# First projections of four RMS-normalized layers fed with un-normalized rows, rotary tables moved, and 20 scaling pieces placed later

## What is computed

```
x = x + conformer_conv_mixer(rms_norm(x, a_norm[0]), ...)      # a0
x = x + forgetting_attention_mixer(rms_norm(x, b_norm), ...)   # b
x = x + short_conv_mixer(rms_norm(x, c_norm), ...)             # c
x = x + conformer_conv_mixer(rms_norm(x, a_norm[1]), ...)      # a1
for l in range(2):                                             # m0 f0 m1 f1
    mod = silu(c) @ w_ada[l] + b_ada[l]          # scale, shift, gate vectors
    x = layer_norm(ALPHA * x + g1 * token_mixer(x * (1 + sc1) + sh1, ...))
    x = layer_norm(ALPHA * x + g2 * conv_ffn(x * (1 + sc2) + sh2, ...))
```

## Time and profile before

| | before |
|---|---|
| median of 3 runs | 1755.38 us (1754.99 to 1758.14) |
| the profiled execution | 1757.02 us, span 1755.1 us |
| PE busy | 1723.7 us (98%) |
| DVE busy | 1477.8 us (84%) |
| ACT busy | 1093.9 us (62%) |
| POOL busy | 289.3 us (16%) |
| DMA | 339.49 MB, mean 193 GB/s |

### The profile page before, as it was taken

The page is one execution under the profiler, slowest core; times in us unless marked ns, Lnnn a source line. Parts: engine busy times, 40 slices in busy tenths (PEclk is TensorE's granted clock), DMA queues, the critical chain, the costliest instruction groups (busy, mean ns, idle before and its releaser), DMA issues.

```text
span 1755.1 us, 28782 instructions
## 1 busy us (share of the span) xinstructions
PE 1723.7 (98%) x10458; PEld 1510.9 (86%) x10458; DVE 1477.8 (84%) x2862; ACT 1093.9 (62%) x2150; POOL 289.3 (16%) x396
## 2 busy tenths in 40 slices
PE   9999999999999999999999999999999999999997
PEld 8888888888888888788898988988888998988886
DVE  7998878877789999888987698789987688789887
ACT  6888665555455555577876455566566656566664
POOL 3996000000000000088920000002000200002000
PEclk9999999999999999999999999999999999999999
DMA  6455568855559888544465654546764544546662
GB/s 240 153 157 174 168 220 304 268 177 184 201 195 315 292 301 309 177 151 144 145 196 157 233 172 133 172 150 187 258 218 144 168 156 130 172 144 187 221 187 78
DMA packets 92734, 339.49 MB, mean 193 GB/s; under 512 B 10288, under 2 KB 10672, under 8 KB 91952
## 3 DMA queue, kind: packets, MB, share of 16 engines
q1 hardware_dynamic: 92592, 337.64, 59.1%
HBM read 336.55 MB, written 1.05 MB: 192 GB/s over the span
## 4 chain that ended last, share of the span: by engine, by line
PE 74%; DVE 12%; ACT 8%; issue 4%; POOL 2%; ACTq 0%; DVEq 0%; POOLq 0%
PE ps L104 72%; DVE wl L120 4%; ACT tmp L110 3%; ACT wh L113 2%; POOL B L120 2%; PE ps L107 2%; DVE tmp L130 1%; DVE raw L130 1%; DVE tmp L120 1%; DVE B L120 1%; ACT os L113 1%; DVE sm L142 1%; DVE os L120 1%; ACT B L110 0%; DVE tmp L125 0%
## 5 line engine op out<-in xcount | busy, mean ns | idle before, releaser
L104 PE MATMUL ps<-XS,wh 128*128 128x256 f32 (+2 forms) x3184 | 780.7, 328 | 8.5 <-DVE wl L120 4.4
L120 DVE TENSOR_TENSOR wl<-raw,wh 128x1024 fp32r<-128x1024 f32 x471 | 576.6, 1238 | 101.4 <-ACT wh L113 99.1
L104 PE MATMUL ps<-XS,wl 128*128 128x256 f32 x2152 | 583.1, 282 | 0.0
L104 PEld LDWEIGHTS ps<-XS,wh 128*128 128x128 f32 (+1 forms) x3184 | 527.0, 191 | 64.9 <-issue 19.0
L113 ACT CAST wh<-raw 128x1024 fp32r<-128x1024 f32 x471 | 479.3, 1044 | 100.3 <-PE ps L104 92.8
L104 PEld LDWEIGHTS ps<-XS,wl 128*128 128x128 f32 x2152 | 409.4, 190 | 11.4
L120 POOL TENSOR_TENSOR B<-B,tmp 128x236 f32<-128x236 f32 (+11 forms) x368 | 247.0, 712 | 640.0 <-ACT tmp L110 625.1
L104 PE MATMUL ps<-wh,os 128*128 128x512 f32 x864 | 280.2, 392 | 4.1 <-DVE os L120 2.8
L130 DVE SCALAR_TENSOR_TENSOR ps<-B,C,ps 128x253 f32<-128x253 f32 (+17 forms) x560 | 216.5, 472 | 2.8 <-ACT ps L110 2.8
L104 PE MATMUL ps<-B,raw 128*128 128x256 f32 x992 | 218.6, 380 | 0.0
L104 PEld LDWEIGHTS ps<-B,raw 128*128 128x128 f32 x992 | 187.0, 190 | 27.2 <-issue 2.9
(11 more groups left out here) (168 smaller groups left out, 1659.7 us busy)
## 6 DMA issues: line engine op xcount, KB each, us to landing
raw<-in_w SPq DMA_DIRECT2D x628, 512.0 KB, 4.4
B<-in_ln SPq DMA_DIRECT2D x4, 1024.0 KB, 7.7
C<-in_cst SPq DMA_DIRECT2D x1, 1103.5 KB, 9.0
X<-in_x SPq DMA_DIRECT2D x2, 512.0 KB, 4.5
out_x<-X SPq DMA_DIRECT2D x4, 256.0 KB, 2.5
cb<-in_cb SPq DMA_DIRECT2D x1, 512.0 KB, 13.6
pos<-in_pos SPq DMA_DIRECT2D x1, 160.0 KB, 5.3
raw<-in_w SPq DMA_DIRECT2D x1, 128.0 KB, 2.0
```

What stands on the lines that cost most here:

```text
L104: return NOTHING if self.e is None else self.e.matmul(*a, **k)
L120: return NOTHING if self.e is None else self.e.tensor_tensor(o, a, b, op)
```

## The change

- Entry of b, c and a1: the quarters of the layer before are finished in the order (0,0), (1,0), (0,1), (1,1). Ahead of the last one PE transposes the first four feature blocks of the *un-normalized* rows, and the other four are transposed inside the first unit. The fillers of these entries go, and 6 of the 24 at the start of a0. The normalizing of the rows ahead of the transposes goes too.
- a0 and a1: g0 (two plain units) is made from the un-normalized rows times the gain; DVE multiplies its result by R. R is spread over the partitions with two matmuls (`pe_row_root`), ACT copies it to SBUF, and DVE makes the normalized blocks from the un-normalized ones. v0 of a1 becomes plain.
- b: v0 comes ahead of b.f and takes un-normalized high and low parts; R is applied as its result leaves PSUM. The same eight blocks are then made again, normalized and split, for v1 and the rest. b.f goes behind v1, and the small work on its result moves to the chunks v2 and k0.
- c: the c and u units of the first step take un-normalized rows; their product is multiplied by R*R. The blocks are made again, normalized and split, for the b and z units.
- The masks of a0 (four) are made ahead of the convolution and not within its first step. The rotary tables are made on DVE and ACT behind output pieces of a1 and not at the start of a0.
- Scaling pieces: 31 instead of 36 in b, 38 instead of 46 in c (fewer at its start, and in its last step two instead of six), 12 instead of 8 in m0 (one behind each of iq0 to iq3 too), 4 instead of 6 in f0 (at steps 18 and 20 instead of 8 to 12), 11 instead of none in m1 (behind iq0 to iq2 and qk0 to qk7).

The diff, cut to its core:

```diff
     for p in range(8):
-        first = "split" if j else "plain"
-        two("g", p, E, *[first if p == 1 else "plain"] * 2)
-        two("v", p, 0, "split" if p else first, "plain" if p else first)
+        two("g", p, E, *["split" if j and p == 1 else "plain"] * 2)
+        two("v", p, 0, "split" if p else "plain", "plain")
         if p in EARLY_Z:
             out += z_unit(EARLY_Z.index(p))
     for x in range(len(EARLY_Z), 16):
...
-    out = [("b.f", [("b_w_in", 0, 128 * k, 128, 4 * E, 16) for k in range(8) for _ in range(2)], "split")]
+    out = []
     u = iter(range(48))
 
     def chunk(which, n, base, adas, kps=range(4)):
                 out.append(ada_piece(0, next(u)))
 
     for n in range(3):
-        chunk("v", n, 2 * E, (1, 2, 3) if n else (3,))
+        chunk("v", n, 2 * E, (1, 2, 3) if n == 2 else ())
+        if n == 1:
+            out.append(("b.f", [("b_w_in", 0, 128 * k, 128, 4 * E, 16) for k in range(8) for _ in range(2)], "split"))
     for which, base in (("k", E), ("q", 0)):
         for n in range(4):
-            chunk(which, n, base, (1, 3))
+            chunk(which, n, base, (1, 3) if which == "q" or n else (3,))
     chunk("v", 3, 2 * E, (1,), range(2))
     for h in range(18):
         if h < 16:
...
             for n in range(2):
                 for kind, base in (("c", 2 * E), ("u", 0)):
                     out.append((f"c.{kind}0.{n}", tiles("c_w_in", 0, base + n * 128), "split"))
-                    if kind == "u":
-                        ada()
         for kind, base in (("c", 2 * E), ("u", 0), ("b", E), ("z", 3 * E)):
             if i == 0 and kind in "cu":
                 continue
             if kind == "z" and i >= 2:
                 out.append((f"c.o{i - 2}", [("c_w_out", 0, 128 * (i - 2), 128, 0, D)], "split"))
-                ada()
+                if i < 14:
+                    ada()
             for n in range(2):
                 out.append((f"c.{kind}{i}.{n}", tiles("c_w_in", 0, base + (i + n) * 128), "split"))
             if kind == "z" and i >= 2:
                 out.append((f"c.o{i - 1}", [("c_w_out", 0, 128 * (i - 1), 128, 0, D)], "split"))
+                if i < 14:
+                    ada()
+            if i and (i < 14 or kind in "cu"):
                 ada()
-            ada()
...
+        if n < (3 if l else 4):
+            ada()
     for n in range(2):
         one(f"cq{n}", tiles(w, l, O_CQ + 128 * n))
...
-            a = next(u, None) if i >= 8 else None
+            a = next(u, None) if i >= 18 else None
             if a is not None:
...
+                if name == "c.u0.0":
+                    pe.wait_ge(*self.s["xlow"][X, max(k, 1)])
...
+            if X == "c" and k < 4:
+                self.pe_raw_turned(pe, "c", k + 4)
...
+    def quarters(self, L):
+
+        return ((0, 0), (1, 0), (0, 1), (1, 1)) if L in ("a0", "b", "c") else ((0, 0), (0, 1), (1, 0), (1, 1))
+
     def out_last(self, pe, L, ks, Ys):
 
-        for tb in range(2):
-            for h in range(2):
-                for k, Y in zip(ks, Ys):
-                    ins = self.out_part(pe, L, k, ks[-1] + 1, Y, tb, h)
-                    names = [(L, "sum", tb, h)] if k == ks[-1] else []
-                    if tb and h:
-                        names += [self.at[f"{L}.o{k}"], (L, "out", k)]
-                    if names:
-                        ins.then_inc(self.s["gemm"].up(*names), 1)
+        for tb, h in self.quarters(L):
+            if tb and h and L in ("a0", "b", "c"):
+                for k in range(4):
+                    self.pe_raw_turned(pe, {"a0": "b", "b": "c", "c": "a1"}[L], k)
+            for k, Y in zip(ks, Ys):
+                ins = self.out_part(pe, L, k, ks[-1] + 1, Y, tb, h)
+                names = [(L, "sum", tb, h)] if k == ks[-1] else []
+                if tb and h:
+                    names += [self.at[f"{L}.o{k}"], (L, "out", k)]
+                if names:
+                    ins.then_inc(self.s["gemm"].up(*names), 1)
...
+        if L[0] in "abc":
+            return [((k + 4) % 8, 0) for k in range(8)]
...
-        self.warm(pe, {"a0": 0, "a1": 14, "b": 15, "c": 16, "m0": 0, "m1": 18}.get(L, 11))
+        if L != "m0":
+            self.warm(pe, 18 if L == "m1" else 11)
...
+    def pe_raw_turned(self, pe, L, k):
+        s, h, a = self.s, k // 4, (k % 4) * 128
+        if L != "a0" and k >= 4:
+            pe.wait_ge(*s["resid"][self.prior(L), 1, 1])
+        for tb in range(2):
+            pe.wait_ge(*(s[f"x{tb}"][0] if L == "a0" else s["resid"][self.prior(L), tb, h]))
+            ins = pe.transpose(self.turned_tile(L, k)[:, tb * 128:tb * 128 + 128], self.half(tb, h)[:, a:a + 128],
+                               self.c("ident", 0, 128))
+        ins.then_inc(s["turn"].up((L, "in", k)), 1)
+
+    def pe_row_root(self, pe, L):
+        pe.wait_ge(*self.s["shift"][L, "raw", 3])
+        pe.wait_ge(*self.s["norm"][L, "root"])
+        self.spread(pe, 7, self.sums("R"), (L, "R"))
...
+    def act_taken(self, act, L, k):
+        act.wait_ge(*(self.s["turn"][L, "in", k] if L[0] == "a" else self.s["xlow"][L, k]))
+        act.activation(self.taken(k), self.turned_tile(L, k), ACT.Identity, scale=self.gain_column(L, k)).then_inc(
+            self.s["shift"].up((L, "raw", k)), 1)
...
+    def dve_joined(self, dve, L, k):
+        dve.wait_ge(*self.s["xlow"][L, k])
+        dve.tt(self.taken(k), self.xh(k).bitcast(F32), self.xl(k).bitcast(F32), ALU.add).then_inc(
+            self.s["norm"].up((L, "raw", k)), 1)
+
+    def dve_normed(self, dve, L, k):
+        dve.wait_ge(*self.s["norm" if k < 2 else "shift"][L, "raw", k])
+        dve.tt(self.taken(k), self.taken(k), self.row_root(), ALU.mult).then_inc(self.s["norm"].up((L, "xn", k)), 1)
+
+    def act_normed_high(self, act, L, k):
+        act.wait_ge(*self.s["norm"][L, "xn", k])
+        act.wait_ge(*(self.s["gemm"]["b.v0", k // 2] if L == "b" else self.s["gemm"]["c", "read", k]))
+        act.copy(self.xh(k), self.taken(k)).then_inc(self.s["high"].up((L + "n", k)), 1)
+
+    def dve_normed_low(self, dve, L, k):
+        dve.wait_ge(*self.s["high"][L + "n", k])
+        dve.tt(self.xl(k), self.taken(k), self.xh(k).bitcast(F32), ALU.subtract).then_inc(
+            self.s["xlow"].up((L + "n", k)), 1)
...
-            for _ in range(24):
+            for _ in range(18):
                 pe.matmul(self.ps[5][:, 0:128], w, w, start=True, stop=True)
             pe.wait_ge(*s["const0"][0])
-        self.pe_entry(pe, A, self.xnt)
+            for k in range(8):
+                self.pe_raw_turned(pe, A, k)
...
+        def taken(n, k):
+
+            pe.wait_ge(*s["norm" if k in (1, 2) else "shift"][A, "raw", k])
+            i = self.at[f"{A}.g0.{n}"]
+            return pe.matmul(self.ps[4][:, n * T:n * T + T], self.raw(i)[:, k * 128:(k + 1) * 128], self.taken(k),
+                             start=k == 0, stop=k == 7)
+
+        def first_gates():
+            for n in range(2):
+                pe.wait_ge(*self.landed(self.at[f"{A}.g0.{n}"]))
+                for k in range(8):
+                    ins = taken(n, k)
+                    if n == 0 and k == 3:
+                        if j:
+                            for late in range(4, 8):
+                                self.pe_raw_turned(pe, A, late)
+                        else:
+                            self.pe_row_root(pe, A)
+                ins.then_inc(s["gemm"].up(self.at[f"{A}.g0.{n}"], f"{A}.g0.{n}"), 1)
+                if j and n == 0:
+                    self.pe_row_root(pe, A)
...
+            self.act_square(act, A, 0, 0)
+            self.act_square(act, A, 0, 1)
+            self.act_square(act, A, 1, 0)
+            self.act_taken(act, A, 0)
+            self.act_taken(act, A, 3)
+            self.act_root(act, self.sums("d"), self.sums("v"), A)
+            for k in range(4, 8):
+                self.act_taken(act, A, k)
+            self.act_row_root(act, A)
+            highs()
...
+            if j and i == 18:
+                self.act_rope(act)
...
-            self.dve_residual(dve, "c")
-        self.dve_rms(dve, A, f"a_norm{j}", True)
+            self.dve_residual(dve, "c", 0, 0)
+            self.dve_residual(dve, "c", 1, 0)
+            self.dve_residual(dve, "c", 0, 1)
+        for k in (1, 2):
+            self.dve_taken(dve, A, k)
+        if j:
+            self.dve_residual(dve, "c", 1, 1)
+        self.dve_first_squares(dve, A)
+        self.dve_all_squares(dve, A)
+        self.dve_row_root(dve, A)
         if j == 0:
-            self.dve_rope(dve)
             self.dve_bias_begin(dve)
+        Rb, g0 = self.row_root(), self.tmp[0].rearrange("p (a t) -> p a t", a=2)
+        dve.wait_ge(*s["evac"][A, "R"])
+        for k in range(8):
+            dve.wait_ge(*s["norm" if k in (1, 2) else "shift"][A, "raw", k])
+            dve.tt(self.xn()[:, k, :], self.taken(k), Rb, ALU.mult).then_inc(s["norm"].up((A, "xn", k)), 1)
+        dve.wait_ge(*s["gemm"][f"{A}.g0.1"])
```

(98 more changed lines are left out.)

353 lines of the change are left out of this document (221 added, 132 removed).

## The result

| | before | after |
|---|---|---|
| median | 1756.09 us (4 runs, 1754.99 to 1758.14) | 1767.74 us (4 runs, 1766.32 to 1769.27) |
| ratio, 95% interval | | 1.0066 [1.0054, 1.0078] |

What follows compares the result with a forecast made beforehand. PE (98% busy) was taken as the bound, so gains came from fewer fillers, stalls and clock falls. Terms summed to 7.3 us, taking the median 1755.4 to 1748.1 us (chance 0.43, 1745 to 1751.5); range 1742 to 1755.

Steps and rivals of the forecast that it cites:

- a0, start: Start of a0: transposes follow 18 fillers without waiting, less 0.5 us for spreading R; gain 1.45 us.
- a0, stall and fall: Ahead of z5 in a0: earlier convolution end removes the 1.94 us stall and the 1.5 us half-clock fall behind it.
- b: Entry of b: 5.6 us before the first unit shrinks to needed transposes, spreading R and short waits; gain 2.25 us.
- c, start and end: c: start gains 1.2 us after 1.7 us of new waits; two stalls at the end go, 2.8 us.
- a1: Entry of a1: 2.8 us saved, 1.35 us given back through v0 becoming plain; gain 1.45 us.
- m0, entry: Entry of m0: rotary-angle and sine work on DVE delays the first residual; first unit 0.95 us later, bounds 0 and 2.75.
- m0, iq: m0 at iq3: only one split piece prepared ahead, giving 0.3 us of stall.
- f0: f0: two stalls of 0.45 us at steps with scaling pieces become one; gain 0.45 us.
- m1, iq and qk: m1: 0.3 us of stall at iq3, plus m0's four stalls and fall at qk, 2.7 + 1.5 us; loss 4.5 us.
- The two new waits: Start of c: PE waits for b0.1's low part and z0.0 for the product c*u, 0.85 us each, bounds 0 and 3 together.
- Scaling pieces later: m0, m1 and f0: moved scaling pieces, which LOOK counts, cost 4.35 us together; bounds for m1 0 and 7.
- The rival on the other side: m0 and m1: shallow look-ahead puts seven iq pieces on PE's path, 1.14 us each; 13 us lost, 1761 us, chance 0.10.

Runs made afterwards that it cites:

- the helper: Code change making the look-ahead of ACT's casts and DVE's low parts in m0 and m1 pass over scaling pieces; in the changed kernel 1746.02 us.
- the helper alone: The kernel before with the look-ahead of m0 and m1 passing over scaling pieces, nothing else changed: 1753.00 us, ratio 0.9977.
- places alone: The kernel before with the scaling pieces at the changed kernel's places and nothing else: 1774.94 us, ratio 1.0108.
- the first helper kernel: The changed kernel with the look-ahead in m0 and m1 passing over scaling pieces, every piece at the same place: 1746.02 us, ratio 0.9945.
- the piece behind iq1 alone: The changed kernel without scaling pieces at iq except one behind iq1 in each of m0 and m1, old look-ahead: 1754.53 us, ratio 0.9989.
- the fastest: The changed kernel with look-ahead passing over scaling pieces in m and f layers, 14 pieces in f0 and one in m1: 1743.55 us, ratio 0.9932.

## Why the prediction was wrong

The marks used are the first residual of a layer on DVE, and a z unit in the middle of a0:

```profile
222.34 2.05 DVE L120 TENSOR_TENSOR X<-X,ps 128x512 f32<-128x512 f32 x3 [1.04 <-PE ps L104]
495.72 1.88 DVE L120 TENSOR_TENSOR X<-X,ps 128x512 f32<-128x512 f32 x3
729.58 1.88 DVE L120 TENSOR_TENSOR X<-X,ps 128x512 f32<-128x512 f32 x3
```

```profile
217.91 2.06 DVE L120 TENSOR_TENSOR X<-X,ps 128x512 f32<-128x512 f32 x3 [1.03 <-PE ps L104]
489.52 1.88 DVE L120 TENSOR_TENSOR X<-X,ps 128x512 f32<-128x512 f32 x3
716.83 2.05 DVE L120 TENSOR_TENSOR X<-X,ps 128x512 f32<-128x512 f32 x3 [3.48 <-PE ps L104]
```

| step | predicted gain | measured | from |
|---|---|---|---|
| a0, start | 1.45 | 1.69 | z unit at 151.91 and 150.22 |
| a0, stall and fall | 3.44 | 2.74 | 222.34 - 217.91 less 1.69 |
| b | 2.25 | 1.77 | 495.72 - 489.52 less 4.43 |
| c, start and end | 4.0 | 6.55 | 729.58 - 716.83 less 6.20 |
| a1 | 1.45 | 1.35 | unit at 855.40 and 841.30 less 12.75 |
| m0, entry | -0.95 | -1.31 | 953.47 - 940.68 less 14.10 |
| m0, iq | -0.3 | -9.31 | stage rows |
| f0 | 0.45 | 0.50 | stage rows |
| m1, iq and qk | -4.5 | -16.35 | stage rows |
| sum | 7.3 | -12.4 | |

**Right:** the first six steps, 11.6 us forecast and 12.8 measured. The nearness of the two sums is in part luck: a0's stall and the entry of m0 fell short and c gave more. In a0 PE's fillers ended at 7.3 us, the transposes at 9.0. val(0) starts at 25.10, as forecast. But the convolution's end came 2.9 us earlier (162.74 to 159.81) and not 5, so the stall before z5 shrank to 0.70 us and did not vanish:

```profile
159.81 0.41 PE L104 MATMUL ps<-B,C 128*32 128x256 f32 x2 [0.70 <-ACT tmp L110]
```

The measured 2.74 of a0 is then 1.24 of stall and 1.5 of clock, and the clock's part is luck: the profile of before happened to have a fall there (last section).

c was mis-sized, on the good side: in its middle an output piece starts 8.3 us early (590.57 against 598.86), so the start gave 2.1 where I took 1.2, and the end 4.5 where I took 2.8. The two new waits that I had worked out for the start are there, smaller, 0.26 and 0.61 us instead of 0.85 each; that is 0.8 of the start's 0.9. At the end both stalls went, 2.8 us; the other 1.7 no experiment splits up, though a part is the mark itself: before, DVE came to the first residual without idle time, after, it had waited there 3.48 us for PE. m1's waits at qk came as in m0 before, 3.9 us (1.79, 0.72, 0.19, 0.44, 0.76) and one fall, for the 2.7 and 1.5 forecast. Two small slips in the working: v0 gives back 1.2 us by its own rows (7.07 less 749.26 - 743.4), where 1.35 is written, and 0.43, 0.20 and a third of 0.22 make 0.70, not 0.72.

**Wrong: one step, "Scaling pieces later".** It says that with a piece in every second place "only one split piece is prepared ahead", and then prices that by the chain from iq1's result to iq3: copy, cast, low part. That chain is what feeds iq3 once things run. I didn't write out which call issues the cast and the low part of iq1 and iq2, nor what stands ahead of that call on ACT and DVE. Both facts were in the code and in the trace of before: ACT's 1.92-us broadcast that waits for DVE, and DVE's copy of iw that waits for PE. The term of 0.3 us a layer was in fact 5.63 us of waiting a layer and three stretches at half clock beside it. Of m0's 9.31 us, 5.66 are idle and 3.65 clock (one of the four stretches, that in the entry, isn't iq's); of m1's 16.35, 9.52 and 6.83, the waits at qk and their fall among them.

The rival on the other side had the right part of the kernel and the right word, a shallow look-ahead in m0 and m1, and 1761 us. Its mechanism was another: each of seven pieces with 1.14 us on PE's path for lack of landed pieces. The pieces had landed: the ones at 950.62 and 960.03 ran without idle time of DVE ahead of them. Still, a piece's own time is on PE's path in places: 1.15 us of the 2.64 ahead of iq2 and the 1.12 that the helper leaves ahead of iq1. The rival's point of decision was so a question that the trace couldn't answer, where the real one, what is queued ahead of iq1's cast, could have been read off. The chance of 0.10 came from that.

What is left open: how m1's waits at qk share out between look-ahead and the pieces' time. With the helper one of them was exchanged for a wait on another operand, and only taking the pieces out brought m1 from 206.7 to 202.9.

## What to carry to other kernels

When work in a list is put between items that a look-ahead counts, write out for each following item which call issues its preparation now, and what that call stands behind on each engine; a wait for something unrelated ahead of it is the price, not the time of the inserted work. Moving optional work out of a full stretch and where it lands are two changes: price and try them apart. Where a kernel gains in many places and still comes out slower, compare the starts of its stages first; that shows in one table which change to keep.

## What the runs showed of the hardware

A fall of the clock isn't a fixed price of a wait. a0's code is the same in the kernel before and in the one with the helper alone. Before, a wait of 1.94 us ahead of z5 had 3.41 us at 0.50 behind it; in places alone, with the same a0, the wait was 1.75 us and no fall came. With the helper the wait was 2.00 us and the clock stayed at 1.00; PE's wait, then the windows over it and behind it:

```profile
162.93 0.41 PE L104 MATMUL ps<-B,C 128*32 128x256 f32 x2 [2.00 <-ACT tmp L110]
...
161.00:164.40 3.40, 1.47 (x15) 1.09 (x16) 2.96 (x3) 1.89 (x4) 0.30 (x1) 1.00 0.32 116
164.40:168.00 3.60, 3.60 (x33) 3.60 (x32) 1.87 (x6) 3.09 (x5) 0.00 (x0) 1.00 0.91 272
```

Likewise the wait of 1.35 or 1.36 us at m0's entry stands in six profiles: a fall follows in three (the changed kernel, the first helper kernel, the piece behind iq1 alone) and none in the other three, the fastest among them. So the 1.5 us that I credited for a0's fall are those of one profiled execution; of three profiles with that a0, one shows it. The list of times points the same way: of the 68 executions of the kernel before that were taken beside the experiments, 34 have a mean clock of 0.996 and took 1757.2 us on average, 28 have 0.997 and took 1755.4, and six have 0.998 and took 1753.8.

The Trainium skill (TensorE: Matmul & The Clock Gate, What's actually happening) says of a kernel's start that the number of slow matmuls differs from run to run of one kernel; the falls in mid-kernel differ here too, as shown. For the size of one: m0 of the changed kernel has four times 3.41 us at half clock and is 206.22 us busy, that of the fastest has none and 200.54, so one costs 5.68/4 = 1.4 us, near the 1.5 estimated.

The four mask products took 4.30 us together before, beside a busy POOL, and 2.49 us in their new place, where no POOL work ran. The windows over them, before and after (POOL is the last of the engines):

```profile
36.62:40.92 4.30, 4.30 (x22) 3.79 (x21) 4.30 (x6) 1.86 (x5) 4.30 (x5) 1.00 0.35 97
```

```profile
19.89:22.38 2.49, 2.49 (x13) 2.21 (x12) 2.49 (x5) 2.36 (x3) 0.00 (x0) 1.00 0.73 222
...
19.89 2.49 DVE L120 TENSOR_TENSOR B<-B 128x512 bf16<-128x512 f32 x4
```

The Trainium skill (GPSIMD Engine Reference, Specifications) says that DVE instructions with two SBUF inputs contend with GpSimd's access, and these rows agree. So the move took 4.3 us out of DVE's full stretch, as forecast, and put only 2.5 us in where it landed: 1.8 us less work in all, which the forecast didn't have.
